# Moving the SBUF tiles of a two-block transformer kernel to multiples of 512 and 64 bytes

## What is computed

```python
# first block
u  = rmsnorm(h) @ w_in                      # 1024 x 7168: q, k, v, xr, gr, ga, gb
ya = chunked_band_attention(q, k, v) @ w_attn_out
yb = (rg_lru(conv(xr)) * gelu(gr)) @ w_rnn_out
h  = h + (sigmoid(ga) * ya + sigmoid(gb) * yb) @ w_o
h  = h + (silu(g) * up) @ w_ffn_out         # g, up = split(rmsnorm(h) @ w_ffn_in), width 2816
# second block
h  = h + 0.5 * rmsnorm(swiglu(rmsnorm(h), ffn1_w_gu, ffn1_w_down))
z  = rmsnorm(h) @ w_in_2                    # neighbourhood attention and latent attention from z
h  = h + rmsnorm(concat(o_na, o_mla) @ w_out_2)
h  = h + 0.5 * rmsnorm(swiglu(rmsnorm(h), ffn2_w_gu, ffn2_w_down))
```

## The kernel before

| tile | offset before | modulo 512 | modulo 64 | offset after | modulo 512 |
|---|---|---|---|---|---|
| `w_raw`, `w_hi`, `w_lo` | 16512, 32896, 49280 | 128 | 0 | 16896, 33280, 49664 | 0 |
| `h` (the stream) | 65664 | 128 | 0 | 66048 | 0 |
| `xt_hi`, `xt_lo` | 73856, 82048 | 128 | 0 | 74240, 82432 | 0 |
| `yt_hi`, `yt_lo` | 152288, 160480 | 224 | 32 | 153088, 161280 | 0 |
| `hid_hi`, `hid_lo` | 94944, 117472 | 224 | 32 | 95744, 118272 | 0 |
| `c_hi`, `c_lo` | 103136, 106208 | 224 | 32 | 103936, 107008 | 0 |
| `u`, `f`, `row_gain`, `sb2`, `pt2` | 94944, 148192, ... | 224 | 32 | 95744, 148992, ... | 0 |
| `grT`, `qkT`, `q_stage`, `sb1`, `pt1` | 168800, ... | 352 | 32 | 169600, ... | 128 |

## Time and profile before

### The profile page before, as it was taken

One profiled execution on the slowest core, in us unless ns is written; L12 is line 12 of the kernel. 1 busy time (PEld: TensorE's weight loads), 2 busy tenths in 40 slices (PEclk: granted clock), 3 DMA queues, 4 the chain that ended last, 5 costly groups with the idle time before them and its releaser, 6 DMA issues.

```text
span 1022.8 us, 13894 instructions
## 1 busy us (share of the span) xinstructions
PE 968.5 (95%) x4535; PEld 795.9 (78%) x4535; DVE 513.8 (50%) x816; ACT 487.8 (48%) x766; POOL 417.7 (41%) x201
## 2 busy tenths in 40 slices
PE   6995887999999999999999999998999989999997
PEld 4874676888878888888878888886878868888886
DVE  3359688543554434442473444237568584434322
ACT  5341664564445444444554454336436464444442
POOL 4445253333434343434444343653521244444442
PEclk9997998999999999999999999999999999999999
DMA  6753344544545565778656565653622337565652
GB/s 224 229 173 99 110 144 137 160 141 126 181 149 182 176 194 179 226 230 233 188 170 195 178 193 180 185 174 103 198 81 63 103 102 218 175 198 171 191 182 78
DMA packets 133264, 169.28 MB, mean 166 GB/s; under 512 B 17723, under 2 KB 88926, under 8 KB 133094
## 3 DMA queue, kind: packets, MB, share of 16 engines
q1 hardware_dynamic: 132038, 168.67, 53.7%
q10 hardware_dynamic: 1184, 0.07, 0.1%
HBM read 167.61 MB, written 1.10 MB: 165 GB/s over the span
## 4 chain that ended last, share of the span: by engine, by line
PE 80%; DVE 12%; ACT 3%; issue 3%; DMA 1%; POOL 0%; DVEq 0%; ACTq 0%; POOLq 0%; SPq 0%
PE acc L780 24%; PE acc L782 24%; PE acc L781 24%; PE tp L825 4%; DVE w_lo L1147 2%; DVE u L1238 2%; DVE h L1525 1%; PE acc L1084 1%; PE sc L1042 1%; PE sc L898 1%; DMA gain_x<-in_norm_mix_g 1%; ACT w_hi L455 1%; DVE u L1235 1%; DVE u L1298 1%; DVE u L1197 0%
## 5 line engine op out<-in xcount | busy, mean ns | idle before, releaser
L1749 POOL TENSOR_TENSOR w_lo<-w_raw,w_hi 128x1024 fp32r<-128x1024 f32 x152 | 374.2, 2462 | 541.9 <-ACT w_hi L455 541.7
L455 ACT ACTIVATE w_hi<-w_raw 128x1024 fp32r<-128x1024 f32 x305 | 322.5, 1060 | 412.2 <-PE acc L782 392.9
L780 PE MATMUL acc<-w_hi,xt_hi 128*128 128x512 f32 (+1 forms) x880 | 352.8, 401 | 14.8 <-DVE w_lo L1147 13.7
L1147 DVE TENSOR_TENSOR w_lo<-w_raw,w_hi 128x1024 fp32r<-128x1024 f32 x153 | 204.0, 1334 | 315.3 <-ACT w_hi L455 313.5
L782 PE MATMUL acc<-w_lo,xt_hi 128*128 128x512 f32 (+1 forms) x880 | 345.0, 392 | 0.0
L781 PE MATMUL acc<-w_hi,xt_lo 128*128 128x512 f32 (+1 forms) x880 | 344.5, 391 | 0.0
L780 PEld LDWEIGHTS acc<-w_hi,xt_hi 128*128 128x128 f32 x880 | 167.4, 190 | 50.3 <-DVE w_lo L1147 15.1
L782 PEld LDWEIGHTS acc<-w_lo,xt_hi 128*128 128x128 f32 x880 | 166.8, 190 | 35.4
L781 PEld LDWEIGHTS acc<-w_hi,xt_lo 128*128 128x128 f32 x880 | 167.5, 190 | 32.7
L780 PE MATMUL acc<-w_hi,hid_hi 128*128 128x512 f32 x264 | 105.6, 400 | 0.0
L781 PE MATMUL acc<-w_hi,hid_lo 128*128 128x512 f32 x264 | 105.1, 398 | 0.0
(11 more groups left out here) (195 smaller groups left out, 822.3 us busy)
## 6 DMA issues: line engine op xcount, KB each, us to landing
w_raw<-in_ffn_w_gu SPq DMA_DIRECT2D x176, 256.0 KB
w_raw<-in_w_in SPq DMA_DIRECT2D x68, 512.0 KB
w_raw<-in_w_ffn_in SPq DMA_DIRECT2D x88, 256.0 KB
w_raw<-in_ffn_w_down SPq DMA_DIRECT2D x44, 512.0 KB
w_raw<-in_w_ffn_out SPq DMA_DIRECT2D x22, 512.0 KB
w_raw<-in_w_rnn_out SPq DMA_DIRECT2D x8, 512.0 KB
w_raw<-in_w_attn_out SPq DMA_DIRECT2D x8, 512.0 KB
w_raw<-in_w_o SPq DMA_DIRECT2D x8, 512.0 KB
```

The source lines that it names most:

```text
L455: act.activation(w_hi[:, b, :], w_raw[:, b, :], ACT.Copy).then_inc(hi_done[b], 1)
L780: pe.matmul(o, hi[:, k, rows], wh, start=first and n == 0, stop=False)
L1147: dve.tensor_tensor(w_lo[:, b, :], w_raw[:, b, :], w_hi[:, b, :].bitcast(F32), ALU.subtract).then_inc(lo_done[b], 1)
L1749: pool.tensor_tensor(w_lo[:, b, :], w_raw[:, b, :], w_hi[:, b, :].bitcast(F32), ALU.subtract).then_inc(lo_done[b], 1)
```

## The change

Three lines of `build` are changed. The first tile starts 384 bytes higher, at 16896 = 33 x 512; each tile of 2 KB and more starts at the next multiple of 64; and `base`, where the two shared sets of tiles begin, is rounded up to a multiple of 512. No instruction is added, removed or put in another order on any engine; operands' addresses alone differ.

```diff
-    top = [16512]
+    top = [16896]
 
     def place(name, shape, dt, at=None):
         size = int(np.prod(shape[1:])) * (2 if dt == BF16 else 4)
         size = (size + 31) // 32 * 32
         if at is None:
+            if size >= 2048:
+                top[0] = (top[0] + 63) // 64 * 64
             at = top[0]
             top[0] += size
         return nc.alloc_sbuf_tensor_at(name, shape, dt, offset=at)
...
-    base = top[0]
+    base = top[0] = (top[0] + 511) // 512 * 512
```

## The result

Five runs of the changed kernel take 1016.26 us in the median (1015.63 to 1016.39), five of the kernel before 1022.75 us (1020.44 to 1024.94): a ratio of 0.9942, 95% interval 0.9928 to 0.9957, so 4.4 to 7.4 us are gained. The prediction was 1015.5 us, with a range of 1012.3 to 1020.7.

The account below looks back on a forecast made before the run. TensorE, busy 968.5 of 1022.8 us, was taken as the bound. Moving `hid`, `yt` and `c` was to gain 7.4 us, everything else nothing: 1022.95 - 7.4 = 1015.5 us, range 1012.3 to 1020.7.

Parts of the forecast that it names:

- What bounds the kernel: Whole kernel: TensorE, busy 968.5 of 1022.8 us; starts of split-product matmuls lie 226.7 ns apart with `xt`, 234 otherwise.
- The price of one matmul and their number: Split products with `hid`, `yt`, `c`: 1008 matmuls, each to gain 7.4 ns, together 7.5 us, taken as 7.4.
- Stationary tiles to multiples of 512: `hid`, `yt` and `c`, moved through `base`, come down to the spacing of `xt`: 7.4 us gained.
- fourth rival: All products: moving and stationary reads meet at multiples of 512; `xt` slows, 19.2 us lost, 1042 us; chance 0.04.
- first rival: `yt`, `hid`, `c`: distance from the rings or region is the cause, so no change, about 1022.9 us; chance 0.08.
- Rings and `xt` to 0 modulo 512 at nothing: Rings and `xt` moved from 128: stay on multiples of 64, their distance unchanged, so nothing gained or lost.
- The gain reaches the end: Output stages: slabs are ready ahead of TensorE, loads and GpSimd stay below their limit, so all 7.4 us arrive.
- The other engines and the loads at nothing: VectorE, ScalarE, GpSimd and DMA: no gain or loss taken; 0.4 us kept in the range for DMA.
- That the phase is not the cause: `yt`, `hid`, `c` stay at 234 ns after the change, time about 1022.9 us; chance 0.08.
- That the 512 itself brings more: All 3600 matmuls come down toward 213.3 ns: 967 us at the end, anything under 1012 us; chance 0.06.
- That common phase hurts: All products: moving and stationary operands both at multiples of 512 make the kernel slower, 1042 us; chance 0.04.

Follow-up runs that it names:

- e1: Kernel before with only `base` rounded up, so `yt`, `hid` and `c` start at a multiple of 64: 1022.85 us, ratio 0.9991.
- e3: Kernel before with all tiles moved 32 bytes higher: 1022.67 us, ratio 0.9992.
- e7: Kernel before with only `base` raised to 128 modulo 512, the phase of the rings and `xt`: 1017.75 us, ratio 0.9950.
- e8: Kernel before with rings and all stationary tiles put at 160 modulo 512: 1016.93 us, ratio 0.9948.
- e2: Kernel before with only the rings, the stream and `xt` moved to multiples of 512: 1022.43 us, ratio 0.9995.
- e9: Changed kernel with stationary tiles shifted from the rings: `xt` 256, `yt` 192, `hid` 384, `c` 320 bytes: 1022.97 us, one run.
- e4: Kernel before with the rings 32 bytes off a multiple of 64 and all stationary tiles on one: 1036.39 us, ratio 1.0116.
- e5: Changed kernel with `xt` 64 bytes further and `hid`, `yt`, `c` beginning 16, 48, 8 bytes into their tiles: 1034.63 us, one run.
- e6: Changed kernel with `hid_hi` at `base` + 32, `hid_lo` 64 past a multiple of 512, `yt_lo` 32 bytes further: 1021.62 us, one run.

## Why the prediction was right, and where its reason was wrong

The time was right and so was the size of the term that makes it; the cause that it named was not, and that the time came out all the same is luck.

**What bounds the kernel: right.** The distance between starts, not the length by line, was the view that showed it. In the change the lengths moved too, by less than 3%: 400 to 391 ns for `hid` and 412 to 406 for `yt` on the first of the three lines.

**The price of one matmul and their number: right.** 7.4 ns were forecast for each of 1008; the traces show 234.3 to 226.7 for `hid` and 234.2 to 226.7 for `yt`; the few with `c` fell less, from 233.9 to 229.0. The time fell by 6.5 us where 7.4 were forecast, and 7.4 is the edge of the interval. A part of the difference: in the trace after, the first matmuls behind a switch of tiles still lie further apart than the later ones, so that with them the mean with `yt` fell by 6.6 ns only (234.3 to 227.7, distances under 300 ns).

**Stationary tiles to multiples of 512: the step that failed.** The prediction said: all three pairs that lie off a multiple of 64 show 234, and the one pair that lies on it shows 226.7. That was read as a cause, and e1 and e3 show that it is none. The four pairs differed in a second thing that went together with the first: `xt` lay 0 modulo 256 from the rings, the others 96. What the runs show in place of the alignment is this distance: 0 modulo 256 gives 226.7 ns at any alignment tried (e7, e8), anything else 229.0 to 234.3. The prediction even held the clue. Its fourth rival says that `xt` and the rings already share one phase modulo 512 and are the fast pair, and uses it only to make that rival unlikely. Its first rival names the distance from the rings and concludes that all would stay at 234, though the change itself brings that distance to 0 modulo 512. Because it does, both readings forecast the same time: that is the luck, and only other placements tell them apart.

**Rings and `xt` to 0 modulo 512 at nothing: right for this part alone, but it can't be left out.** The sum took nothing since the distance of `xt` from the rings stays; e2 shows 0.9995. But the 7.4 us don't belong to the stationary tiles alone, either: with the rings left at 128, a `base` at a multiple of 512 would lie 384 from them, where `hid` takes 233.3 ns (e9). The two parts bring the gain only together.

**The gain reaches the end: right.** f1o and f3o became 1.9 us shorter each where about 2 were forecast, `rnn` and `o` 0.6 each where 0.7 were. ScalarE's wait for TensorE in f1o stayed (29.5 us), and no wait for slabs took its place.

**The other engines and the loads at nothing: right.** VectorE's split takes 686 ns with `xt` and 683 with `yt` after the change; the first product begins anywhere between 12.3 and 14.8 us in the traces, with no order by where the tiles lie.

**The rivals.** That the phase is not the cause was given 0.08, as a rival in which nothing changes. It was half true: the phase modulo 64 is not the cause, and the time changed all the same. That the 512 itself brings more: no mean lies under 226.7 ns at any distance tried. The Trainium skill ("TensorE: Matmul & The Clock Gate", Wait — 56ns, not 53.3ns?) gives 215.7 ns for back-to-back matmuls of 512 columns at the full clock; none of these products reaches it. That common phase hurts: the opposite holds, and its price, 19.2 us if `xt` loses the rings' phase, is of the order of the 13.3 us that e4 lost against the kernel before. The Trainium skill ("SBUF — State Buffer", Specifications) gives SBUF lines of 16 bytes. They don't account for the price either: `xt` at a distance of 64 bytes, a whole number of such lines, costs 6.6 ns more than at 0 (e5).

## What to carry to other kernels

Where TensorE is the bound and each float32r matmul loads a new stationary tile, put stationary and moving tiles at the same address modulo 256; that is worth some 3% of these matmuls here, and where the address itself lies doesn't matter (0, 128 and 160 modulo 512 were tried). To find such a price, look at the distance between starts in the timeline, within one kernel, between operands that are placed differently. And when such a comparison names a cause, list what else separates the two sides: the two cheapest experiments here (moving everything by 32 bytes; moving one side alone) would each have refuted the first reading.

## What was not expected of the hardware

- TensorE's rate depends on the distance of two operands' addresses, with a period of 256 bytes: 226.7 ns at 0, 229.0 to 234.3 ns at the seven other distances in the table. Moving all tiles together by 32 bytes changes nothing (0.9992), and the price stays, 234.2 ns, while no other engine and no load is active.
- The dependence isn't smooth: 233.3 ns at 64, 234.3 at 96, 233.3 at 160, 229.0 at 192, 233.3 at 224. A pair with its two tiles at 32 and 64 takes 231.1 (e6), less than either distance by itself.
- At the half clock there is no such price: 427 ns with `yt` as with `xt`.
